# Last-layer MLP: a weight's high and low parts interleaved word by word, and the second up slab's product taken in another column order

## The chip, the cores and the metric

The kernel runs on one core of a Trainium2 chip. The metric is the device time of one execution in microseconds; lower is better.

## The reference

Two transformer layers run one after the other on 512 tokens of width 1024, in float32. The change touches only the end of the second layer, its squared-ReLU MLP with a hidden width of 4096:

```python
def squared_relu_mlp(xn, w_up, w_down):
    return jnp.square(jax.nn.relu(xn @ w_up)) @ w_down

x = x + squared_relu_mlp(rmsnorm_2(x, norm_mlp[l]), w_up[l], w_down[l])   # w_up 1024x4096, w_down 4096x1024
return rmsnorm_2(x, norm_final)
```

## The kernel before

Each operand of a product is split in a high part (`fp32r`, written by ScalarE as a Copy that rounds) and a low part (`fp32r`, VectorE: value minus high part). A product of a 128x128 weight block with a 128x512 activation block is then three matmuls into one PSUM bank (`mm3`, lines 902 to 904): high by high, high by low activation, low weight by high activation. Each matmul carries its own weight load.

Weights come in slabs of 1024x512 words (4096 words in each of the 128 partitions, 2 MB, two DMAs of 1 MB on SyncE's queue) into the two slots of `W` (`weight_slots`). A slab's slot is refilled when the slab two before it is used up. ScalarE then writes the high part in two halves of 2048 words into `W_hi` (`weights_hi`, arena tiles 0 to 15, two slots), and VectorE writes the low part in two halves into `W_lo` (`weight_slots_lo`, two slots). TensorE waits on the semaphore `w_lo` for both halves.

The last layer's MLP runs in MQ = 4 parts. `mlp_part` exists on TensorE, ScalarE and VectorE, and each part has four slabs, n = 0 to 3: two of `w_up` (8 blocks of 128 hidden features, MH = 8) and two of `w_down`. A slab is 4 output banks x KD = 8 blocks of the contraction x 3 matmuls = 96 matmuls, 1536 in all.

- n = 0 goes through `together` (lines 939, 940 and 944), which holds four banks open: first all products with the high activation, then those with the low one.
- n = 1 uses `mm3` with the activations `mlp_hi` and `xn_lo`. In the trace these are the rows of lines 902 to 904 with `mlp_hi` or `xn_lo`.
- n = 2 and 3 use `mm3` with `sq_hi` and `sq_lo`, the squares.

VectorE takes each up bank out of PSUM (line 3289: ReLU times `rstd`), ScalarE squares it into `sq_hi` (line 2399), VectorE squares it again and subtracts (`rsq`, `sq_lo`, lines 3291 and 3294), and adds each down bank to the residual (`part_out`, line 3302). The split of slab s+1 stands in the same program order on ScalarE (line 2394) and VectorE (line 3283): slab n+1 is split while TensorE works on slab n. The very first slab, `("mup", 0)`, is split earlier with `split_w` (lines 1664 and 2435), between the last residual additions of the attention. The DMA of the second slab waits for the job before `mup_0`, which is `norm_sum("norm_mlp")` (line 863), placed in the middle of the first slab's products.

Three lines elsewhere, which the change does not touch, use operands that are not contiguous or much narrower. `exponents` (lines 2925 to 2928, VectorE, levels `lev` = 2, 4, ... 128, twice each) works on views split into runs of `lev // 2` words:

```python
v = v.rearrange("p (n b t) -> p n b t", b=2, t=lev // 2)
return v[:, :, 0], v[:, :, 1]
...
V.tensor_tensor(Al, ref(Fc, 0, hp, lev), Fl, ALU.subtract)          # line 2925
```

so at `lev` = 2 both inputs and the output step by two words. Line 1027 (TensorE) reads its moving operand as `posT[0:33, :].rearrange("p (i e) -> p e i", e=2)[:, e, :]`, every second word; line 1034 reads a contiguous one. Line 1342 is a product with 128 contiguous moving columns and a contiguous 128x128 weight block in plain float32; the trace records two load and matmul pairs for each such product.

Of the kernel before, what the change touches and what calls it, by code (L numbers as in the profile page):

```python
# [13 lines left out]
F32 = mybir.dt.float32  # L14
# [335 lines left out]
def two_blocks(nc, io, out_dram):  # L350
# [10 lines left out]
    with ExitStack() as ctx:  # L361
# [192 lines left out]
        sq_lo, sq_hi = parts("sq_lo", 16, MH), parts("sq_hi", 32, MH)  # L554
# [278 lines left out]
        def _(pe):  # L833
# [776 lines left out]
            def mlp_part(first, q):  # L1610

                for n in range(4):
                    s = s0 + n
                    pe.wait_ge(w_lo, 2 * (w0 + n + 1) + 8 * first + 8 * q)
                    wh, wl = (w[:, s % 2, :].rearrange("p (k c) -> p k c", k=KD) for w in (W_hi, W_lo))
# [9 lines left out]
                    xh, xl = (mlp_hi, xn_lo) if n == 1 else (sq_hi, sq_lo)  # L1625
                    for m, j in enumerate(js):
                        c = slice(P * m, P * m + P)
                        pe.wait_ge(psum_free[j % 8], j // 8 + 2 * first + 2 * q)
                        for k in range(KD):
                            if n == 2 and m == 0:  # L1630

                                pe.wait_ge(sem("sq_lo"), k + 1 + MH * first + MH * q)
                            ins = mm3(PS[j % 8][:], wh[:, k, c], wl[:, k, c], xh[:, k, :], xl[:, k, :], k == 0, k == KD - 1)
                        ins.then_inc(psum_full, 1)
# [10 lines left out]
        def _(act):  # L1645
# [728 lines left out]
            def before_mlp(k):  # L2374
                if k:
                    high_mlp(k - 1)
                if k == KD - 2:
                    split_w("mup", 0)
                evicted(act, f"out3_{k}")
# [7 lines left out]
            def mlp_part(q, last):  # L2387

                for n in range(4):
                    if not (last and n == 3):  # L2390
                        s = s0 + n + 1
                        act.wait_ge(w_landed[s % 2], landings(s) + 64 * q)
                        for a, b in ((0, 2048), (2048, 4096)):
                            A(W_hi[:, s % 2, a:b], W[:, s % 2, a:b], ACT.Copy).then_inc(w_hi, 1)  # L2394
# [13 lines left out]
        def _(dve):  # L2408
# [854 lines left out]
            split_w("mup", 0)  # L3263
# [8 lines left out]
            def mlp_part(q, last):  # L3272


                for n in range(4):
# [3 lines left out]
                    if not (last and n == 3):  # L3279
                        s = s0 + n + 1  # L3280
                        for e, (a, b) in enumerate(((0, 2048), (2048, 4096))):
                            dve.wait_ge(w_hi, 2 * (w0 + n + 1) + e + 1 + 8 * q)
                            V.tensor_tensor(W_lo[:, s % 2, a:b], W[:, s % 2, a:b], W_hi[:, s % 2, a:b].bitcast(F32),  # L3283
                                            ALU.subtract).then_inc(w_lo, 1)
# [236 lines left out]
```

## Time and profile before

| | |
|---|---|
| median of 3 runs | 1660.04 us (1659.95 to 1660.29) |
| span of the profiled execution | 1660.1 us |
| TensorE matmuls busy | 1614.1 us (97%) |
| VectorE / ScalarE / GpSimd busy | 977.3 / 682.4 / 153.4 us |
| mean granted clock of TensorE | 0.993 |
| the four parts of the last MLP, first to last product | 1297.9 to about 1648 us |

The profiled execution has no other time than its span, and that is the median of the runs to 0.1 us. "PEld" rows are the weight loads, which overlap the matmuls. Matmul records overlap one another too: a record of 389 ns does not mean that one matmul starts every 389 ns. The distance from start to start is what counts.

### The profile page before, as it was taken

To read this page: it belongs to the slowest core of one execution; us is meant where nothing else is said; L and a number is where in the kernel's file an instruction comes from. 1 tells how busy PE (TensorE), PEld (TensorE's weight loads), DVE (VectorE), ACT (ScalarE), POOL (GpSimd) and SP (SyncE) were. 2 spreads that over 40 slices of the span, in tenths; PEclk is the share of its full clock that TensorE was granted. 3 is DMA by queue.
4 is the path that set the end of the run, shared out by engine and by line. 5 is a ranking of instruction groups with operands and counts; after the bars stand their busy time and mean duration, and the time that the engine had idled before them with its cause. 6 is when DMAs were issued, how large, how long until landed. Compare 5 with 4: busy or idle time off the path is not lost.

```text
span 1660.1 us, 18984 instructions
## 1 busy us (share of the span) xinstructions
PE 1614.1 (97%) x7258; PEld 1268.9 (76%) x7258; DVE 977.3 (59%) x1411; ACT 682.4 (41%) x1060; POOL 153.4 (9%) x155
## 2 busy tenths in 40 slices
PE   5999999999999999999999999999999999999997
PEld 1488765687788888888888787688877888888885
DVE  6986687784544424436789498675434554435262
ACT  4531465323533213325654667964433322222131
POOL 0221000252000000004000000342001000000001
PEclk9999999999999999999999999999999999999999
DMA  9543114422332232223141121444210322222231
GB/s 311 198 152 127 64 54 162 153 65 89 103 101 89 76 116 84 92 95 133 52 176 56 47 77 36 162 152 153 101 52 28 125 74 83 98 101 101 101 101 51
DMA packets 112600, 173.89 MB, mean 105 GB/s; under 512 B 3851, under 2 KB 56651, under 8 KB 112012
## 3 DMA queue, kind: packets, MB, share of 16 engines
q1 hardware_dynamic: 108220, 158.05, 28.2%
q0 software_dynamic: 4304, 14.81, 2.7%
q8 instruction: 49, 0.80, 0.2%
q14 instruction: 27, 0.22, 0.0%
HBM read 168.53 MB, written 4.33 MB: 104 GB/s over the span
## 4 chain that ended last, share of the span: by engine, by line
PE 84%; DVE 8%; DMA 3%; ACT 2%; issue 2%; SPq 1%; DVEq 0%; ACTq 0%
PE bank L902 17%; PE bank L904 17%; PE bank L903 17%; PE bank L939 6%; PE bank L940 6%; PE bank L944 5%; DMA weight_slots<-in_w_mod 2%; PE bank L1212 2%; PE bank L1132 1%; PE bank L1144 1%; PE bank L1342 1%; DVE weight_slots_lo L2435 1%; PE bank L1432 1%; PE bank L1407 1%; PE bank L1450 1%
## 5 line engine op out<-in xcount | busy, mean ns | idle before, releaser
L3328 POOL TENSOR_TENSOR arena<-arena 128x512 f32<-128x512 f32 (+1 forms) x56 | 76.3, 1371 | 960.3 <-ACT arena L1695 956.8
L904 PE MATMUL bank<-hx_hi,weight_slots_lo 128*128 128x512 f32 x320 | 124.8, 390 | 0.0
L3283 DVE TENSOR_TENSOR weight_slots_lo<-weight_slots,weights_hi 128x2048 fp32r<-128x2048 f32 x30 | 67.4, 2289 | 93.5 <-ACT weights_hi L2394 93.5
L2394 ACT ACTIVATE weights_hi<-weight_slots 128x2048 fp32r<-128x2048 f32 x30 | 55.8, 1908 | 160.6 <-DMA weight_slots<-in_w_up 115.9
L1664 ACT ACTIVATE weights_hi<-weight_slots 128x2048 fp32r<-128x2048 f32 (+2 forms) x46 | 77.3, 1724 | 91.7 <-DMA weight_slots<-in_ffn_w_down 57.9
L903 PE MATMUL bank<-xn_lo,weights_hi 128*128 128x512 f32 x288 | 112.0, 389 | 0.0
L902 PE MATMUL bank<-sq_hi,weights_hi 128*128 128x512 f32 x256 | 99.6, 389 | 0.0
L903 PE MATMUL bank<-sq_lo,weights_hi 128*128 128x512 f32 x256 | 99.6, 389 | 0.0
L904 PE MATMUL bank<-sq_hi,weight_slots_lo 128*128 128x512 f32 x256 | 99.6, 389 | 0.0
L1650 ACT ACTIVATE arena<-bank 128x512 f32<-128x512 f32 (+2 forms) x99 | 49.1, 532 | 96.1 <-PE bank L904 45.0
L2435 DVE TENSOR_TENSOR weight_slots_lo<-weight_slots,weights_hi 128x2048 fp32r<-128x2048 f32 (+2 forms) x34 | 65.8, 1973 | 28.1 <-ACT weights_hi L1664 28.1
L1695 ACT ACTIVATE arena<-arena 128x512 f32<-128x512 f32 (+1 forms) x68 | 38.9, 579 | 101.4 <-DVE arena L3302 28.3
L939 PE MATMUL bank<-xn_hi,weights_hi 128*128 128x512 f32 x192 | 76.3, 397 | 3.1 <-ACT xn_hi L1680 3.1
L2770 DVE TENSOR_TENSOR weight_slots_lo<-weight_slots,weights_hi 128x2048 fp32r<-128x2048 f32 x18 | 40.4, 2288 | 60.5 <-ACT weights_hi L1935 60.5
L940 PE MATMUL bank<-xn_hi,weight_slots_lo 128*128 128x512 f32 x192 | 75.9, 395 | 0.0
L944 PE MATMUL bank<-xn_lo,weights_hi 128*128 128x512 f32 x320 | 74.2, 389 | 0.0
L3302 DVE TENSOR_TENSOR arena<-bank,arena 128x512 f32<-128x512 f32 x32 | 22.1, 690 | 87.3 <-PE bank L904 87.3
L904 PEld LDWEIGHTS bank<-hx_hi,weight_slots_lo 128*128 128x128 f32 x320 | 60.1, 188 | 12.8
L944 PEld LDWEIGHTS bank<-xn_lo,weights_hi 128*128 128x128 f32 x320 | 60.1, 188 | 12.5
L902 PE MATMUL bank<-ff_hi,weights_hi 128*128 128x512 f32 x176 | 68.5, 389 | 0.0
L903 PE MATMUL bank<-ff_lo,weights_hi 128*128 128x512 f32 x176 | 68.5, 389 | 0.0
L904 PE MATMUL bank<-ff_hi,weight_slots_lo 128*128 128x512 f32 x176 | 68.5, 389 | 0.0
(473 smaller groups left out, 4069.6 us busy)
## 6 DMA issues: line engine op xcount, KB each, us to landing
weight_slots<-in_w_in SPq DMA_DIRECT2D x24, 1024.0 KB, 7.3
weight_slots<-in_ffn_w_up SPq DMA_DIRECT2D x22, 1024.0 KB, 6.8
weight_slots<-in_w_up SPq DMA_DIRECT2D x16, 1024.0 KB, 6.6
weight_slots<-in_w_down SPq DMA_DIRECT2D x16, 1024.0 KB, 6.4
weight_slots<-in_w_mod SPq DMA_DIRECT2D x14, 1024.0 KB, 10.2
arena<-in_w_mod POOLq DMA_DIRECT2D x32, 256.0 KB, 3.3
weight_slots<-in_w_out SPq DMA_DIRECT2D x8, 1024.0 KB, 7.8
weight_slots<-in_w_xkv SPq DMA_DIRECT2D x8, 1024.0 KB, 7.6
```

The costliest lines, as they stand in the source:

```text
L902: mm(ps, lh, rh, start=start, stop=False)
L903: mm(ps, lh, rl, start=False, stop=False)
L904: return mm(ps, ll, rh, start=False, stop=stop)
L939: mm(ps[:, 0:width], wh(k, m), x2[0][:, k, 0:width], start=k == 0, stop=False)
L940: mm(ps[:, 0:width], wl(k, m), x2[0][:, k, 0:width], start=False, stop=False)
L944: ins = mm(ps[:, 0:width], wh(k, m), x2[1][:, k, 0:width], start=False, stop=k == KD - 1)
L1650: free(A(out, src, ACT.Copy), name)
L1664: A(high_half(kind, n, i), W[:, s_, a:b], ACT.Copy).then_inc(w_hi, 1)
L2394: A(W_hi[:, s % 2, a:b], W[:, s % 2, a:b], ACT.Copy).then_inc(w_hi, 1)
L2435: V.tensor_tensor(low(kind, n)[:, a:b], W[:, s, a:b], high_half(kind, n, i).bitcast(F32), ALU.subtract).then_inc(w_lo, 1)
L3283: V.tensor_tensor(W_lo[:, s % 2, a:b], W[:, s % 2, a:b], W_hi[:, s % 2, a:b].bitcast(F32), ALU.subtract).then_inc(w_lo, 1)
L3328: G.tensor_tensor(acc, acc, sq[i % 2][:, 0:width], ALU.add).then_inc(sq_added, 1)
```

## The change

For the 16 slabs of this MLP, high and low part of a slab now lie in one tile `W_pair` of 4096 x 2 words: word 2i is the high part of weight i, word 2i + 1 its low part. There are two such tiles (for even and odd slots), in arena tiles 0 to 15 and 32 to 47. `sq_hi` moves from tiles 32 to 39 to tiles 24 to 31. ScalarE writes, and VectorE reads and writes, with a step of two words, and so does every weight load. `W_lo` is no longer used in this MLP. The order of instructions, the semaphores and their counts stay.

For the slabs n = 1, the moving operand and the PSUM output are both read in the order `p (a j b) -> p j a b` with a = 2, j = 64, b = 4: columns 0 to 3, 256 to 259, 4 to 7, 260 to 263 and so on. Each column still goes to its own place in the bank.

```diff
@@ -551,7 +551,10 @@
         pT = tiles(44, 2)
         pbuf = [tile(46), tile(47)]
         ao_lo, ao_hi = parts("ao_lo", 24, 8), parts("ao_hi", 16, 8)
-        sq_lo, sq_hi = parts("sq_lo", 16, MH), parts("sq_hi", 32, MH)
+        sq_lo, sq_hi = parts("sq_lo", 16, MH), parts("sq_hi", 24, MH)
+        first_pair = slabs["mup", 0][0] % 2
+        W_pair = [parts(f"weights_pair_{i}", 32 if i == first_pair else 0, 16).rearrange("p a c -> p (a c)").rearrange(
+            "p (w e) -> p w e", e=2) for i in range(2)]
         relu = [tile(a) for a in range(58, 62)]
         rsq = [tile(80), tile(81)]
 
@@ -1612,7 +1615,7 @@
                 for n in range(4):
                     s = s0 + n
                     pe.wait_ge(w_lo, 2 * (w0 + n + 1) + 8 * first + 8 * q)
-                    wh, wl = (w[:, s % 2, :].rearrange("p (k c) -> p k c", k=KD) for w in (W_hi, W_lo))
+                    wh, wl = (W_pair[s % 2][:, :, e].rearrange("p (k c) -> p k c", k=KD) for e in range(2))
                     js = [j0 + 4 * n + m for m in range(4)]
                     if n == 0:
                         for j in js:
@@ -1623,6 +1626,11 @@
                                  lambda: norm_sum("norm_mlp"), KD if first else 4)
                         continue
                     xh, xl = (mlp_hi, xn_lo) if n == 1 else (sq_hi, sq_lo)
+
+                    def turned(v, n_=n):
+
+                        return v.rearrange("p (a j b) -> p j a b", a=2, b=4) if n_ == 1 else v
+
                     for m, j in enumerate(js):
                         c = slice(P * m, P * m + P)
                         pe.wait_ge(psum_free[j % 8], j // 8 + 2 * first + 2 * q)
@@ -1630,7 +1638,7 @@
                             if n == 2 and m == 0:
 
                                 pe.wait_ge(sem("sq_lo"), k + 1 + MH * first + MH * q)
-                            ins = mm3(PS[j % 8][:], wh[:, k, c], wl[:, k, c], xh[:, k, :], xl[:, k, :], k == 0, k == KD - 1)
+                            ins = mm3(turned(PS[j % 8][:]), wh[:, k, c], wl[:, k, c], turned(xh[:, k, :]), turned(xl[:, k, :]), k == 0, k == KD - 1)
                         ins.then_inc(psum_full, 1)
 
             mlp_part(0, 0)
@@ -2375,7 +2383,10 @@
                 if k:
                     high_mlp(k - 1)
                 if k == KD - 2:
-                    split_w("mup", 0)
+                    s = slabs["mup", 0][0]
+                    act.wait_ge(w_landed[s % 2], landings(s))
+                    for a, b in ((0, 2048), (2048, 4096)):
+                        A(W_pair[s % 2][:, a:b, 0], W[:, s % 2, a:b], ACT.Copy).then_inc(w_hi, 1)
                 evicted(act, f"out3_{k}")
 
             norm_squares("norm_mlp", lambda k: xb[:, k, :], before=before_mlp)
@@ -2391,7 +2402,7 @@
                         s = s0 + n + 1
                         act.wait_ge(w_landed[s % 2], landings(s) + 64 * q)
                         for a, b in ((0, 2048), (2048, 4096)):
-                            A(W_hi[:, s % 2, a:b], W[:, s % 2, a:b], ACT.Copy).then_inc(w_hi, 1)
+                            A(W_pair[s % 2][:, a:b, 0], W[:, s % 2, a:b], ACT.Copy).then_inc(w_hi, 1)
                     for m in range(4 * n, 4 * n + 4) if n < 2 else ():
                         r = relu[m % 4]
                         j = j0 + m
@@ -3260,7 +3271,11 @@
             low_mlp([0, 1, 2, 3])
             residual("out3", [5])
             low_mlp([4])
-            split_w("mup", 0)
+            s = slabs["mup", 0][0]
+            for e, (a, b) in enumerate(((0, 2048), (2048, 4096))):
+                dve.wait_ge(w_hi, 2 * split_no["mup", 0] + e + 1)
+                pair = W_pair[s % 2][:, a:b, :]
+                V.tensor_tensor(pair[:, :, 1], W[:, s % 2, a:b], pair[:, :, 0].bitcast(F32), ALU.subtract).then_inc(w_lo, 1)
             residual("out3", [6])
             low_mlp([5])
             residual("out3", [7])
@@ -3280,8 +3295,8 @@
                         s = s0 + n + 1
                         for e, (a, b) in enumerate(((0, 2048), (2048, 4096))):
                             dve.wait_ge(w_hi, 2 * (w0 + n + 1) + e + 1 + 8 * q)
-                            V.tensor_tensor(W_lo[:, s % 2, a:b], W[:, s % 2, a:b], W_hi[:, s % 2, a:b].bitcast(F32),
-                                            ALU.subtract).then_inc(w_lo, 1)
+                            pair = W_pair[s % 2][:, a:b, :]
+                            V.tensor_tensor(pair[:, :, 1], W[:, s % 2, a:b], pair[:, :, 0].bitcast(F32), ALU.subtract).then_inc(w_lo, 1)
                     if n < 2:
                         for m in range(4 * n, 4 * n + 4):
                             j = j0 + m
```

## Rows read from the trace of the kernel before

**Rows 1.** The page, part 1: busy time, share and instructions of each engine.

```profile
span 1660.1 us, 18984 instructions
PE 1614.1 (97%) x7258; PEld 1268.9 (76%) x7258; DVE 977.3 (59%) x1411; ACT 682.4 (41%) x1060; POOL 153.4 (9%) x155
```

**Rows 2.** One MLP part in windows: length, busy of engines, clock, DMA share.

```profile
core 0: us, PE busy (x) PEld busy (x) DVE busy (x) ACT busy (x) POOL busy (x), PEclk, DMA share, GB/s
1387.00:1474.00 87.00, 87.00 (x386) 72.06 (x385) 39.36 (x41) 19.95 (x16) 0.00 (x0) 1.00 0.29 97
```

**Rows 3.** The chain that ended last, from 1270 us: start, duration, what.

```profile
1306.87 7.85 DMA weight_slots<-in_w_up
1314.75 1.93 ACT weights_hi L2394
1318.90 2.30 DVE weight_slots_lo L3283
...
1401.35 7.25 PE bank L944 x32
...
1575.43 7.25 PE bank L944 x32
```

**Rows 4.** Who waited for whom, TensorE from 1268 us: us, times, longest.

```profile
PE bank L902 <- DVE weight_slots_lo L3283: 0.6, 1, 0.6
```

**Rows 5.** Groups by line, form kept, in the window 1297 to 1650 us.

```profile
L902 PE MATMUL bank<-sq_hi,weights_hi 128*128 128x512 f32 x256 | 99.6, 389 | 0.0
L3283 DVE TENSOR_TENSOR weight_slots_lo<-weight_slots,weights_hi 128x2048 fp32r<-128x2048 f32 x30 | 67.4, 2289 | 93.5 <-ACT weights_hi L2394 93.5
L2394 ACT ACTIVATE weights_hi<-weight_slots 128x2048 fp32r<-128x2048 f32 x30 | 55.8, 1908 | 160.6 <-DMA weight_slots<-in_w_up 115.9 <-DMA weight_slots<-in_w_down 44.7
L902 PEld LDWEIGHTS bank<-sq_hi,weights_hi 128*128 128x128 f32 x256 | 48.1, 188 | 10.0
```

**Rows 6.** Timeline inside slab n = 1: start, duration, engine, line.

```profile
1324.12 0.39 PE L902 MATMUL bank<-mlp_hi,weights_hi 128*128 128x512 f32 x1
1324.12 0.19 PEld L903 LDWEIGHTS bank<-xn_lo,weights_hi 128*128 128x128 f32 x1
1324.35 0.39 PE L903 MATMUL bank<-xn_lo,weights_hi 128*128 128x512 f32 x1
```

**Rows 7.** Timeline of a run of 128-column matmuls, level products of the second layer.

```profile
930.54 1.95 PE L1342 MATMUL bank<-arena 128*128 128x128 f32 x16
930.54 1.75 PEld L1342 LDWEIGHTS bank<-arena 128*128 128x128 f32 x15
```

**Rows 8.** Timeline at the kernel's start: two runs of 256-column matmuls.

```profile
5.36 1.12 PE L1027 MATMUL bank<-arena 33*64 33x256 f32 x4 [5.36 <-DMA arena<-in_hy_w]
10.26 1.12 PE L1034 MATMUL bank<-arena 64*64 64x256 f32 x4 [3.78 <-ACT arena L1733]
```

**Rows 9.** Single lines of VectorE: duration min/median/max, first and last start.

```profile
L2925 DVE TENSOR_TENSOR arena<-arena x14: 676/685/696, 867.1 to 1010.1; 128x512 f32<-128x512 f32 x14
L3294 DVE TENSOR_TENSOR sq_lo<-arena,sq_hi x32: 691/693/696, 1322.6 to 1605.9; 128x512 fp32r<-128x512 f32 x32
```

**Rows 10.** Groups of shorter splits, whole kernel: 1024 words on each engine.

```profile
L2441 DVE TENSOR_TENSOR weight_slots_lo<-weight_slots,weight_slots_lo 128x1024 fp32r<-128x1024 f32 x12 | 14.7, 1222 | 7.3 <-ACT weight_slots_lo L1675 7.3
L1675 ACT ACTIVATE weight_slots_lo<-weight_slots 128x1024 fp32r<-128x1024 f32 x12 | 12.5, 1045 | 0.0
```

**Rows 11.** Timeline before the third up slab: its split, its first product.

```profile
1375.58 4.49 DVE L3283 TENSOR_TENSOR weight_slots_lo<-weight_slots,weights_hi 128x2048 fp32r<-128x2048 f32 x2 [4.33 <-ACT weights_hi L2394]
1386.68 0.39 PE L939 MATMUL bank<-mlp_hi,weights_hi 128*128 128x512 f32 x1
```

**Rows 12.** Timelines around the first slab: its split, and its first product.

```profile
1290.99 3.72 ACT L1664 ACTIVATE weights_hi<-weight_slots 128x2048 fp32r<-128x2048 f32 x2 [1.82 <-DMA weight_slots<-in_w_up]
1292.94 4.49 DVE L2435 TENSOR_TENSOR weight_slots_lo<-weight_slots,weights_hi 128x2048 fp32r<-128x2048 f32 x2 [4.39 <-ACT weights_hi L1664]
1297.87 0.39 PE L939 MATMUL bank<-mlp_hi,weights_hi 128*128 128x512 f32 x1
```


## The prediction, made before the changed kernel ran

> **What bounds the kernel now.** I read the page first: TensorE's matmuls are busy 97% of the span, no other engine above 59% [rows 1]. In the last layer TensorE is busy for the whole of an 87 us window, at a granted clock of 1.00, that is at 2.4 GHz; VectorE has 39 us of work there and ScalarE 20 [rows 2]. The chain that ended last says the same: the low products of slab n = 0 start at 1401.35 and 1575.43 us, two parts of 384 matmuls apart, so 174.08 / 768 = 226.7 ns from matmul to matmul [rows 3]. Nothing but TensorE's own pace is in those parts. Two places are otherwise: the start of the first slab, and the start of the second, where the chain leaves TensorE for the DMA of the slab (it lands at 1314.72), ScalarE's first half and VectorE's two halves [rows 3]. There TensorE waits 0.6 us, its only wait for a split in this layer [rows 4].
>
> So the change can cost time in two ways: by the pace of 1536 matmuls with their loads, or by the splits at those two places. It removes no instruction and no wait.
>
> **The groups and the pace.** One matmul record lasts 389 ns, one weight load 188 ns [rows 5]. The timeline shows how they lie: the load for the next matmul starts with the current matmul (1324.12), lasts 188 ns, and the next matmul starts at 1324.35 [rows 6]. The load is off the path by 226.7 - 188 = 38.7 ns, and the group's idle time agrees (10.0 us over 256 loads is 39 ns) [rows 5]. That is the cover of a slower load.
>
> **Weight loads with a step of two words (1536 of them).** No load in the trace has a step. From below: nothing to gain, since the load is hidden already. From above: a load that needs the time of every word it passes. Its streaming time comes from the 128-column products: 15 loads in 1.75 us from the first start to the last end, so (1.75 - 0.188) / 14 = 111.6 ns from load to load, with the 128-column matmuls between them, and a load streams in no more than that [rows 7]. The rest of its 188 ns is latency that does not repeat. Doubled, a load record would be 188 + 111.6 = 299.6 ns, past the matmul's 226.7 by 72.9 ns even if the next matmul starts the instant the load ends: 1536 x 72.9 = 112.0 us.
>
> Which end? A stepped load passes 2 x 128 words in 111.6 ns, 2.29 words per ns. The moving operand is read at 512 words in 226.7 ns, 2.26 words per ns [rows 3, 7]. Passing memory at that rate is what TensorE's other read does all the time. The nearest row with a step is a moving operand of every second word, line 1027: 4 records in 1.12 us, and the contiguous line 1034, of the same 256 columns, also 1.12 us [rows 8]. Other port, slow start of the kernel, but the step itself cost nothing. I take 0.
>
> **Turned order in the slabs n = 1 (4 slabs x 96 = 384 matmuls).** The moving operand is read, and the bank written, in 128 runs of four words that hop between the two halves of the 512. No row shows a matmul output that is not contiguous. From below 0: no row shows a 512-column product at a shorter pace than 226.7 ns, in whatever place its operands lie. From above: half pace, one more 226.7 ns for each matmul, 384 x 0.2267 = 87.1 us. In between: one lost column slot for each run, 128 x 226.7 / 512 = 56.7 ns a matmul, 21.8 us in all. The number of columns and of matmuls is the same, and the stepped read of line 1027 ran at the contiguous pace [rows 8]; a run of four is milder than a step of two. I take 0 and keep both prices for rivals.
>
> **ScalarE's and VectorE's splits (32 halves each).** VectorE: two inputs and an output with a step of two words occur at level 2 of line 2925; all its 14 executions, over seven levels, lie between 676 and 696 ns, the contiguous 512-word subtraction of line 3294 at 691 to 696 [rows 9]. So VectorE's step costs 0. ScalarE has no stepped write in the trace. From below 0; from above each word twice: 2048 words take 1.908 us and 1024 take 1.045, so 0.843 ns a word, and a half would take 1.73 us more [rows 5, 10]. I take 0, as on VectorE.
>
> What hides a slower split: at a later slab VectorE is done at 1375.58 + 4.49 = 1380.07 and TensorE starts the slab at 1386.68, 6.6 us of slack [rows 11]. At the first slab the split ends at 1292.94 + 4.49 = 1297.43 and the first product starts at 1297.87: 0.44 us of slack [rows 12]. At the second slab there is none, TensorE already waits [rows 4]. Of a split, ScalarE's first half and VectorE's two halves are in the chain. ScalarE doubled costs 1.73 - 0.44 = 1.3 us at the first slab and 1.7 us at the second, 3.0 us together: the DMA of the second slab waits for a job inside the first slab, so the shift carries on and the two add.
>
> **Edits at nothing.** The new homes of the pair tiles and of `sq_hi` only need dead memory; semaphores, their counts and the queues are the same, and no DMA moves. Two buffers alternate by slab parity as before, so no new wait arises.
>
> **Sum.** 0 + 0 + 0 against the profiled execution's own 1660.1 us, which is the runs' median: 1660.0 us. The changes that this kernel's measurement can tell from none are those over 0.2%, 3.3 us.
>
> **Rivals.**
>
> A. *The bank's write order sets the pace.* For: every PSUM write of the trace is contiguous, so nothing vouches for hops. Against: the same columns in the same number. At half pace 1660.0 + 87.1 = 1747.1 us; at one slot for each run 1681.8 us. It decides (over 0.2%) from 3.3 us / 384 = 8.6 ns a matmul on. Chance 0.11, of it 0.05 for the small price.
>
> The Trainium skill speaks against the change here (Advanced Engine Details and Errata, "PSUM Cachelines"): any non-contiguous pattern slows matmuls significantly. Its next line asks only that every two consecutive elements be contiguous, which runs of four fulfil. By the first line rival A holds and the sum goes by its price, up to 1747.1 us; by the second it stays at 1660.0. No row here shows which.
>
> B. *The stepped weight load outgrows its cover.* For: no stepped load in the trace. Against: the rates above. It decides beyond 38.7 + 3.3 / 1.536 = 40.8 ns more a load, a third of its streaming time. At twice the streaming time 1660.0 + 112.0 = 1772.0 us. Chance 0.06.
>
> C. *ScalarE's stepped write is slow.* 1663.0 us if doubled, just inside 0.2%. If VectorE doubled too (2.289 - 1.222 = 1.07 us for 1024 words, so 2.13 us a half), the chain would grow by 1.73 + 4.27 = 6.0 us, still under the 6.6 us of later slabs, and the end would come 5.6 + 6.0 = 11.6 us later, 1671.6 us; its own rows speak against that [rows 9, 10]. Chance 0.04, of it 0.03 within 0.2%.
>
> D. *Faster.* The only slack to win on the chain is the 0.6 us wait, 0.03%. A better placing of operands in memory could shorten the pace of 226.7 ns, but from 2.1 ns a matmul on it would show, and nothing in the window varies. Chance 0.02.
>
> **How the numbers follow.** Forecast, all costs hidden or nil: 0.77. With the small case of C, within 0.2%: 0.80. Slower: 0.11 + 0.06 + 0.01 = 0.18. Faster: 0.02. The range 1658.0 to 1665.0 holds the forecast and C's small case, 0.80; what it leaves out is A, B, C's large case and D. Reaching for A's small price at 1682 would add 0.05 for three times the width.
>
> **What the changed profile would show.** Right: the rows of lines 902 to 904 with `mlp_hi` at 389 ns, weight loads of the last layer at 188 ns with 39 ns of idle each, the low products of n = 0 again 87.04 us apart, the stepped ScalarE and VectorE halves at 1.91 and 2.29 us, 0.6 us of wait at the second slab. Wrong by A: longer matmul records in n = 1 alone, its parts 87 us plus a quarter of the excess. Wrong by B: load records above 227 ns and matmuls of all four slabs apart by as much, n = 2 and 3 too. Wrong by C: longer ScalarE halves and a longer wait at two places only.

## The result: slower by 1.1%

The changed kernel takes 1679.01 us (median; 1677.14 to 1679.21), the kernel before in the same comparison 1659.99 us (1658.47 to 1660.29). The ratio is 1.0111, with a 95% interval of 1.0099 to 1.0123: 19.0 us slower. The forecast was 1660.0 us, with 1665.0 as the upper end.

Part 1 of the page of the changed kernel, which answers to [rows 1]:

```profile
span 1677.2 us, 18984 instructions
PE 1632.6 (97%) x7258; PEld 1278.5 (76%) x7258; DVE 979.6 (58%) x1411; ACT 692.4 (41%) x1060; POOL 154.0 (9%) x155
```

The instructions are the same in number. In this pair of profiled executions TensorE is busy 18.5 us longer, ScalarE 10.0 and VectorE 2.3. The next question is whether the added TensorE time is waiting or pace. The chain that ended last, answering to [rows 3]:

```profile
1312.69 7.47 PE bank L947 x32
1404.56 7.47 PE bank L947 x32
1496.39 7.47 PE bank L947 x32
1588.21 7.47 PE bank L947 x32
```

(Lines 942, 943 and 947 here are lines 939, 940 and 944 of before; 905 to 907 are 902 to 904; ScalarE's split 2394 is 2405 and VectorE's 3283 is 3299.) The low products of n = 0 now stand 91.83 us apart instead of 87.04, 4.79 us more for a part, and a run of 32 takes 7.47 instead of 7.25 us. The first part loses 0.9 us less: from its first product to that of the second part it takes 92.71 us instead of 88.81. Its n = 0 is 0.6 us longer by the pace, and TensorE's wait for the split of the second slab, 0.6 us before [rows 4], is gone (only the load in front of it still waits, 0.2 us, last line of the groups below). From the first product of this MLP to the last it is 368.0 us instead of 349.7 in the two profiled executions, 18.3 us more. (Its first product comes at 1296.76 us against 1297.87; over the other runs that varies from 1295.1 to 1299.1 us.) The loss of 19.0 us, whose interval reaches from 16.4 to 20.4 us, thus lies in the last MLP. Between 1388 and 1476 us the window shows no idle time and the same clock as [rows 2], 1.00, which is 2.4 GHz:

```profile
core 0: us, PE busy (x) PEld busy (x) DVE busy (x) ACT busy (x) POOL busy (x), PEclk, DMA share, GB/s
1388.00:1476.00 88.00, 88.00 (x369) 71.27 (x369) 39.40 (x40) 22.47 (x16) 0.00 (x0) 1.00 0.27 96
```

The groups of the last layer (1297 to 1670 us), answering to [rows 5]:

```profile
L905 PE MATMUL bank<-sq_hi,weights_pair 128*128 128x512 f32 x256 | 100.9, 394 | 0.0
L3299 DVE TENSOR_TENSOR weights_pair<-weight_slots,weights_pair 128x2048 fp32r<-128x2048 f32 x30 | 69.9, 2374 | 97.6 <-ACT weights_pair L2405 97.6
L2405 ACT ACTIVATE weights_pair<-weight_slots 128x2048 fp32r<-128x2048 f32 x30 | 64.9, 2223 | 162.7 <-DMA weight_slots<-in_w_up 116.3 <-DMA weight_slots<-in_w_down 46.4
L905 PE MATMUL bank<-mlp_hi,weights_pair 128*128 128x512 f32 x128 | 53.7, 420 | 0.0
L905 PEld LDWEIGHTS bank<-sq_hi,weights_pair 128*128 128x128 f32 x256 | 49.4, 193 | 10.4
...
L905 PEld LDWEIGHTS bank<-mlp_hi,weights_pair 128*128 128x128 f32 x128 | 25.1, 196 | 7.8 <-DVE weights_pair L3299 0.2
```

The matmul records grow from 389 to 394 ns everywhere, and to 420 ns in n = 1. The weight load takes 193 instead of 188 ns and still has 41 ns of idle time behind it (10.4 us over 256). It is still shorter than its cover, and nevertheless the matmuls are further apart. The timeline at the border of n = 0 and n = 1, answering to [rows 6]:

```profile
1411.63 0.39 PE L947 MATMUL bank<-xn_lo,weights_pair 128*128 128x512 f32 x1
1411.87 0.42 PE L905 MATMUL bank<-mlp_hi,weights_pair 128*128 128x512 f32 x1
1412.12 0.42 PE L906 MATMUL bank<-xn_lo,weights_pair 128*128 128x512 f32 x1
1412.38 0.41 PE L907 MATMUL bank<-mlp_hi,weights_pair 128*128 128x512 f32 x1
1412.62 0.42 PE L905 MATMUL bank<-mlp_hi,weights_pair 128*128 128x512 f32 x1
```

The starts are 0.24 to 0.26 us apart. What I call the **pace** below is the distance of starts averaged over such rows: from the first to the 24th start of an output block of `mm3`, divided by 23, with the starts that the trace keeps to 1 ns (the views print them to 10). The first block of n = 1 in the first part, whose second start comes late, is left out here. Before, the pace is 226.7 ns in all four slabs (n = 0 is counted over its 32 low products). Now it is 233.3 ns in n = 0, 2 and 3 and 256.6 ns in n = 1. That is 4 x (3 x 96 x 6.6 + 96 x 29.9) ns = 19.1 us, and 18.2 us with the 0.9 us that the first part loses less.

ScalarE's and VectorE's halves are longer too. Two halves of each, first in the slab n = 1 and then in n = 2:

```profile
1419.91 5.00 ACT L2405 ACTIVATE weights_pair<-weight_slots 128x2048 fp32r<-128x2048 f32 x2 [5.87 <-DMA weight_slots<-in_w_down]
1446.08 4.07 ACT L2405 ACTIVATE weights_pair<-weight_slots 128x2048 fp32r<-128x2048 f32 x2 [8.03 <-DMA weight_slots<-in_w_down]
...
1422.46 5.12 DVE L3299 TENSOR_TENSOR weights_pair<-weight_slots,weights_pair 128x2048 fp32r<-128x2048 f32 x2 [7.63 <-ACT weights_pair L2405]
1448.18 4.49 DVE L3299 TENSOR_TENSOR weights_pair<-weight_slots,weights_pair 128x2048 fp32r<-128x2048 f32 x2 [5.19 <-ACT weights_pair L2405]
```

Before, a ScalarE pair took 3.72 us and a VectorE pair 4.49 us [rows 11, 12]. The step costs ScalarE 0.18 us a half and VectorE nothing. In the turned slab both are slower again, ScalarE by 0.9 and VectorE by 0.6 us a pair. All of this lies beside other work.

### The profile page after: what moved, and what is told of

It is laid out like the page before. It is cut to its first block, busy times and chain, and to the rows that moved or that the text cites. A ratio compares the mean times of both kernels' runs of the same rounds, so it can differ in the third digit from the quotient of the medians.

```text
span 1677.2 us, 18984 instructions
## 1 busy us (share of the span) xinstructions
PE 1632.6 (97%) x7258; PEld 1278.5 (76%) x7258; DVE 979.6 (58%) x1411; ACT 692.4 (41%) x1060; POOL 154.0 (9%) x155
## 4 chain that ended last, share of the span: by engine, by line
PE 87%; DVE 8%; DMA 2%; ACT 1%; issue 1%; SPq 1%; DVEq 0%; ACTq 0%
PE bank L905 17%; PE bank L907 17%; PE bank L906 17%; PE bank L942 6%; PE bank L943 6%; PE bank L947 5%; PE bank L1215 2%; PE bank L1135 1%; PE bank L1147 1%; PE bank L1065 1%; PE bank L1345 1%; PE bank L1435 1%; DMA weight_slots<-in_w_mod 1%; PE bank L1410 1%; DVE weight_slots_lo L2446 1%
## 5 line engine op out<-in xcount | busy, mean ns | idle before, releaser
L2405 ACT ACTIVATE weights_pair<-weight_slots 128x2048 fp32r<-128x2048 f32 x30 | 64.9, 2223 | 162.7 <-DMA weight_slots<-in_w_up 116.3
L3299 DVE TENSOR_TENSOR weights_pair<-weight_slots,weights_pair 128x2048 fp32r<-128x2048 f32 x30 | 69.9, 2374 | 97.6 <-ACT weights_pair L2405 97.6
L907 PE MATMUL bank<-hx_hi,weight_slots_lo 128*128 128x512 f32 x320 | 124.8, 390 | 0.0
L1672 ACT ACTIVATE weights_hi<-weight_slots 128x2048 fp32r<-128x2048 f32 (+2 forms) x44 | 73.6, 1715 | 88.9 <-DMA weight_slots<-in_ffn_w_down 57.2
L907 PE MATMUL bank<-sq_hi,weights_pair 128*128 128x512 f32 x256 | 100.9, 394 | 0.0
L905 PE MATMUL bank<-sq_hi,weights_pair 128*128 128x512 f32 x256 | 100.9, 394 | 0.0
L906 PE MATMUL bank<-sq_lo,weights_pair 128*128 128x512 f32 x256 | 100.9, 394 | 0.0
L942 PE MATMUL bank<-xn_hi,weights_hi 128*128 128x512 f32 x192 | 75.6, 394 | 3.1 <-ACT xn_hi L1688 3.1
L2781 DVE TENSOR_TENSOR weight_slots_lo<-weight_slots,weights_hi 128x2048 fp32r<-128x2048 f32 x18 | 40.4, 2288 | 59.7 <-ACT weights_hi L1943 59.7
L2446 DVE TENSOR_TENSOR weight_slots_lo<-weight_slots,weights_hi 128x2048 fp32r<-128x2048 f32 (+2 forms) x32 | 61.3, 1953 | 23.2 <-ACT weights_hi L1672 23.0
L905 PE MATMUL bank<-hx_hi,weight_slots_lo 128*128 128x512 f32 x160 | 64.7, 405 | 1.0 <-DVE weight_slots_lo L2452 1.0
L906 PE MATMUL bank<-hx_lo,weight_slots_lo 128*128 128x512 f32 x160 | 62.3, 389 | 0.0
L905 PE MATMUL bank<-xn_hi,weights_hi 128*128 128x512 f32 x160 | 62.2, 389 | 0.0
```

Source lines behind the costliest of these rows:

```text
L905: mm(ps, lh, rh, start=start, stop=False)
L906: mm(ps, lh, rl, start=False, stop=False)
L907: return mm(ps, ll, rh, start=False, stop=stop)
L942: mm(ps[:, 0:width], wh(k, m), x2[0][:, k, 0:width], start=k == 0, stop=False)
L1672: A(high_half(kind, n, i), W[:, s_, a:b], ACT.Copy).then_inc(w_hi, 1)
L2405: A(W_pair[s % 2][:, a:b, 0], W[:, s % 2, a:b], ACT.Copy).then_inc(w_hi, 1)
```

## The experiments

### One part at a time

**e1_pair_only**: the interleaved pair with everything that belongs to it, in plain column order.

```diff
-    ins = mm3(turned(PS[j % 8][:]), wh[:, k, c], wl[:, k, c], turned(xh[:, k, :]), turned(xl[:, k, :]), ...)
+    ins = mm3(PS[j % 8][:], wh[:, k, c], wl[:, k, c], xh[:, k, :], xl[:, k, :], ...)     # against the changed kernel
```

> The changed kernel with its second up slabs in the plain column order; only the word-by-word interleaving is left. In the changed kernel matmuls of slabs n = 0, 2, 3 follow one another every 233.3 ns, 6.6 ns more than before. Theory 'two separate costs, the stepped weight load in the path': all 1536 matmuls take 6.6 ns more, n = 1 too, so 1660.0 + 10.2 = 1670.2 us. Rival 'the interleaving only hurts through ScalarE and VectorE working on the same words': the pace is longer only where these two work. Rival 'the load is hidden as predicted, the turned slabs disturb the rest': 1660 us.

**e2_turned_only**: the turned order on the kernel before, with its separate high and low tiles.

```diff
-    ins = mm3(PS[j % 8][:], wh[:, k, c], wl[:, k, c], xh[:, k, :], xl[:, k, :], ...)
+    ins = mm3(turned(PS[j % 8][:]), wh[:, k, c], wl[:, k, c], turned(xh[:, k, :]), turned(xl[:, k, :]), ...)
```

> The kernel before with only the turned column order in the second up slabs; weights contiguous. In the changed kernel these 384 matmuls follow every 256.5 ns. Theory 'two separate costs that add': 256.5 - 6.6 = 249.9 ns each, 384 x 23.2 = 8.9 us more, 1668.9 us. Rival 'the slower of two sets the pace': 256.5 ns alone as well, 384 x 29.8 = 11.4 us more, 1671.4 us.

Measured: e1 1669.31 us, ratio 1.0051 (1.0037 to 1.0065); e2 1669.44 us, ratio 1.0056 (1.0043 to 1.0070). The kernel before on the same chip took 1660.76 us. The product of the two ratios is 1.0107; the whole change has 1.0111. The pace says where: in e1 it is 233.3 ns in every slab, in e2 250.1 ns in n = 1 and 226.7 ns elsewhere. So the two costs are 6.6 ns for each of 1536 matmuls (10.2 us) and 23.4 ns for each of 384 (9.0 us). They add up, also where they meet: 226.7 + 6.6 + 23.4 = 256.7, measured 256.6. Groups of e1:

```profile
L2405 ACT ACTIVATE weights_pair<-weight_slots 128x2048 fp32r<-128x2048 f32 x30 | 61.3, 2096 | 162.2 <-DMA weight_slots<-in_w_up 116.0 <-DMA weight_slots<-in_w_down 46.2
L905 PE MATMUL bank<-mlp_hi,weights_pair 128*128 128x512 f32 x128 | 50.5, 395 | 0.0
L905 PEld LDWEIGHTS bank<-mlp_hi,weights_pair 128*128 128x128 f32 x128 | 24.7, 193 | 5.5 <-DVE weights_pair L3299 0.3
```

and of e2:

```profile
L2398 ACT ACTIVATE weights_hi<-weight_slots 128x2048 fp32r<-128x2048 f32 x30 | 56.5, 1932 | 159.6 <-DMA weight_slots<-in_w_up 115.4 <-DMA weight_slots<-in_w_down 44.2
L902 PE MATMUL bank<-mlp_hi,weights_hi 128*128 128x512 f32 x128 | 53.3, 416 | 0.2 <-DVE weight_slots_lo L3287 0.2
L902 PEld LDWEIGHTS bank<-mlp_hi,weights_hi 128*128 128x128 f32 x128 | 24.2, 189 | 8.2 <-DVE weight_slots_lo L3287 0.6
```

In e2 the load record is as before (189 ns) while the matmul record has grown to 416: the turned order slows the matmul and not the load. ScalarE's split is slightly slower there too (1932 against 1908 ns) though its own operands are contiguous.

### Which side of the turned matmul: e3_turned_read, e4_turned_write

```diff
-    ins = mm3(PS[j % 8][:], wh[:, k, c], wl[:, k, c], xh[:, k, :], xl[:, k, :], ...)
+    ins = mm3(PS[j % 8][:], wh[:, k, c], wl[:, k, c], turned(xh[:, k, :]), turned(xl[:, k, :]), ...)   # e3
+    ins = mm3(turned(PS[j % 8][:]), wh[:, k, c], wl[:, k, c], xh[:, k, :], xl[:, k, :], ...)           # e4
```

> The kernel before, with only the moving operand of the second up slabs read in the turned order; the bank is written contiguously, so these slabs' columns land in other places. Theory 'the PSUM write of hopping runs costs' (rival A of the prediction): 226.7 ns as before, 1660.0 us. Rival 'the read of the moving operand costs': all of what the turned order costs, about 250 ns a matmul, 1669 us.

> The kernel before, with only the PSUM output of the second up slabs written in the turned order; the moving operand is read contiguously, so these slabs' columns land in other places. Theory 'the PSUM write costs': about 250 ns a matmul, 1669 us. Rival 'the read costs': 226.7 ns, 1660.0 us. If both sides cost a part, each of the two runs shows its part.

Measured: e3 1670.17 us, e4 1660.91 us, before 1660.76 us. The pace of n = 1 is 250.1 ns in e3, exactly e2's, and 226.7 ns in e4. The chain and the group of e4:

```profile
1400.37 7.25 PE bank L944 x32
1487.40 7.25 PE bank L944 x32
...
L902 PE MATMUL bank<-mlp_hi,weights_hi 128*128 128x512 f32 x128 | 49.9, 390 | 0.0
```

Its parts are 87.03 us apart, as in [rows 3]. Writing a bank in 128 hopping runs of four words is free; reading the moving operand so is the whole cost. Of the two lines of the Trainium skill that the prediction weighed (Advanced Engine Details and Errata, "PSUM Cachelines"), this measurement agrees with the second, on pairs of elements, and not with the first, on any non-contiguous pattern.

### What in the read costs: e7, e8, e11, e12

These change the order in which n = 1 reads its 512 moving words. They are e3 with other numbers in `p (a j b) -> p j a b`: runs of b words, taken in turn from a places.

```diff
+    v.rearrange("p (a j b) -> p j a b", a=64, b=4)            # e7: runs of 4, 32 bytes apart
+    v.rearrange("p (a j b) -> p j a b", a=2, b=8)             # e8: runs of 8, hop 1 KB
+    a, b = ((0, 0), (4, 4), (16, 4), (2, 0))[m]               # e11; m = 0: hop 1008 bytes, m = 3: every second word
+    a, b = ((2, 2), (2, 16), (2, 32), (2, 64))[m]             # e12: runs of 2, 16, 32, 64, hop 1 KB
```

> The kernel before, the moving operand of slabs n = 1 read in runs of four words at a distance of eight words, in two sweeps (the bank is written contiguously, columns land elsewhere). Again 128 runs, but no hop of 1 KB. Theory 'every break between runs costs': 250.1 ns a matmul, 1669 us. Rival 'the hop between the two halves, 1 KB apart, costs': 226.7 ns, 1660 us.

> The kernel before, the moving operand of slabs n = 1 read in runs of eight words that hop between the halves (64 runs; the bank is written contiguously). Theory 'every break between runs costs the same': half of 23.4 ns, 238.4 ns a matmul, 1664.5 us. Rival 'the three-dimensional pattern itself costs': 250.1 ns. Rival 'runs shorter than eight words are the trouble': 226.7 ns.

> The kernel before, moving operand of slabs n = 1 read in runs of four words in four ways, one for each output block (bank written contiguously, columns land elsewhere). m = 0: hops of 1008 bytes instead of 1024; m = 1: four places 512 bytes apart in turn; m = 2: sixteen places 128 bytes apart in turn; m = 3: no runs, every second word, in two sweeps. Theory 'two reads at a power-of-two distance meet in the same part of the memory': m = 0 near the 231.1 ns of the 32-byte distance, m = 1 and 2 at 250 ns or more. Rival 'any break costs by how far it jumps': m = 0 at 250.1, m = 1 below it, m = 2 near 231. m = 3: by the Trainium skill's rule of two accesses a line 226.7 ns; if every further line costs as in the weight load's case, 233 ns or more.

> The kernel before, moving operand of slabs n = 1 read in runs that hop between the halves, the run length by output block: 2, 16, 32 and 64 words for m = 0, 1, 2, 3 (256, 32, 16 and 8 runs; bank written contiguously, columns land elsewhere). Runs of four cost 23.4 ns a matmul (128 runs), runs of eight 16.6 (64 runs, 0.26 ns each). Theory 'a fixed cost for a hop that short runs partly hide': 16 words 32 x 0.26 = 8.3 ns, 235.0; 32 words 230.9; 64 words 228.8; 2 words above 250. Rival 'a three-dimensional pattern has a fixed cost beside it': the last three converge on a value above 226.7 ns.

Measured: e7 1662.25 us (before 1660.78), e8 1669.18 (1660.78), e11 1689.22 and e12 1671.88 (1659.99). The paces of n = 1, with what each is above 226.7 ns:

| run of words | distance of the runs | pace, ns | more |
|---|---|---|---|
| 4 | 32 bytes, ascending | 231.1 | 4.4 |
| 4 | 128 bytes, 16 places | 247.3 | 20.6 |
| 4 | 512 bytes, 4 places | 267.5 | 40.8 |
| 4 | 1008 bytes, 2 places | 243.2 | 16.5 |
| 4 | 1024 bytes, 2 places | 250.1 | 23.4 |
| 8 | 1024 bytes, 2 places | 243.3 | 16.6 |
| 16 / 32 / 64 | 1024 bytes, 2 places | 240.5 / 236.8 / 228.7 | 13.8 / 10.1 / 2.0 |
| 2 | 1024 bytes, 2 places | 339 | 112 |
| 1, every second word | 8 bytes | 450.7 | 224.0 |

(The 231.1 ns of e7 hold for parts 1 to 3; in its part 0 the pace is 233.3.) The last line of the table, seen in the timeline of e11 at the border of the blocks m = 2 and m = 3:

```profile
1431.62 0.42 PE L903 MATMUL bank<-xn_lo,weights_hi 128*128 128x512 f32 x1
1431.87 0.41 PE L904 MATMUL bank<-mlp_hi,weight_slots_lo 128*128 128x512 f32 x1
1432.12 0.62 PE L902 MATMUL bank<-mlp_hi,weights_hi 128*128 128x512 f32 x1
1432.56 0.63 PE L903 MATMUL bank<-xn_lo,weights_hi 128*128 128x512 f32 x1
```

A moving operand of every second word takes twice the time (450.7 / 226.7 = 1.99). This is the very pattern that the prediction took for free from line 1027. Runs of 4 words, which are 16 bytes, cost 2% at the shortest distance and 7 to 18% at the others; runs below 16 bytes cost half as much again or all of it again. Longer hopping runs cost less, but not in proportion to the number of hops: 128 runs cost 23.4 ns, 64 cost 16.6, 32 cost 13.8. No price per hop fits, and the sums written down before the runs missed: 238.4 ns for runs of 8 (243.3), 235.0 for 16 (240.5), 230.9 for 32 (236.8), while 228.8 for 64 came true (228.7); and at 1008 bytes either 231.1 or 250.1 (243.2). The Trainium skill (Advanced Engine Details and Errata, "SBUF Cachelines") wants at least two hits on a 16-byte line for full performance. For the moving operand this measurement differs: every second word has two hits on each line and takes twice the time.

### The stepped load: e5, e6, e10, e14

**e5_load_step4** leaves all writes of ScalarE and VectorE contiguous and lets TensorE alone read its weights with a step of four words. **e6_load_64** loads half as many weight columns. **e10_steps** reads with steps of 3, 4, 5 and 8 words in the four blocks of each slab.

```diff
+    def stepped(w, k, m):                                                   # e5, all four slabs
+        return w.rearrange("p (k c e) -> p k c e", k=KD, e=4)[:, k, :, m]
+    mm3(PS[j % 8][0:64, :], wh[:, k, P * m:P * m + 64], wl[:, k, P * m:P * m + 64], ...)     # e6, n = 1, 2, 3
+    def stepped(w, k, m, step):                                             # e10, e9, e13, e15
+        at = min(512 * k, 4096 - P * step)
+        return w[:, at:at + P * step].rearrange("p (c e) -> p c e", e=step)[:, :, 0]
+    sh, sl = (stepped(w, k, m, (3, 4, 5, 8)[m]) for w in wide)              # e10, n = 1, 2, 3
```

> The kernel before: ScalarE and VectorE write high and low parts contiguously as ever, but all 1536 weight loads of the MLP read their 128 words with a step of four (the hidden features come out in another order). Step two cost 6.6 ns a matmul. Theory 'the load pays by the distance it passes': three extra words for each where step two had one, 3 x 6.6 = 19.9 ns, 246.6 ns a matmul, 1690.6 us. Rival 'the loads only suffered from ScalarE and VectorE working word by word on the same tile': 226.7 ns, 1660 us. Rival 'what counts is how many words of a 16-byte line are used' (Trainium skill, SBUF): one of four is past its limit, a far larger cost than three times step two's.

> The kernel before, but the 1152 matmuls of slabs n = 1, 2, 3 load only 64 of their 128 weight columns (half of the output rows are left out). Theory 'the load is in the path, a matmul starts some 39 ns after its load has ended': the load is half its streaming time shorter, up to 55.8 ns, and the pace falls below 226.7 ns, until something else holds it; down to 213.3 ns (512 columns at 2.4 GHz) it would give 1152 x 13.4 = 15.4 us, 1644.6 us. Rival 'the matmul sets the pace and the load hides behind it, as predicted': 226.7 ns, 1660 us.

> The kernel before, loads in slabs n = 1, 2, 3 with a step of 3, 4, 5 and 8 words for output blocks m = 0, 1, 2, 3 (other weights than the reference's), tiles written contiguously. Theory 'from a step of four on every word is a line of its own and the load itself takes 235 ns': 235.0 ns for steps 4, 5 and 8, and between 233.3 and 235.0 for step 3. Rival 'the distance passed counts': more for 5 and more again for 8. Whole: about 1660.8 + 1152 x 0.0083 = 1670.4 us.

Measured: e5 1671.21 us and e6 1663.42 us against 1660.78; e10 1675.74 against 1659.99. Groups of e5:

```profile
L902 PE MATMUL bank<-mlp_hi,weights_hi 128*128 128x512 f32 x128 | 50.9, 398 | 0.0
L902 PEld LDWEIGHTS bank<-mlp_hi,weights_hi 128*128 128x128 f32 x128 | 39.6, 310 | 0.0
```

At a step of four words the load record is 310 ns with no idle time, and the pace is 234.9 ns, not the 246.6 that three times the price of step 2 would give. Here the load has outgrown its cover, as rival B had it, at a larger step: e15 below puts the load's own time at 233.3 ns. The steps 3, 4, 5 and 8 of e10 give 235.7, 235.2, 236.7 and 246.6 ns. Groups of e6:

```profile
L902 PE MATMUL bank<-mlp_hi,weights_hi 128*64 128x512 f32 x128 | 50.3, 393 | 0.2 <-DVE weight_slots_lo L3283 0.2
L902 PEld LDWEIGHTS bank<-mlp_hi,weights_hi 128*64 128x64 f32 x128 | 17.1, 134 | 12.8 <-DVE weight_slots_lo L3283 0.6
```

A load that is 54 ns shorter brings nothing: the pace is 230.0 ns, even 3.3 ns more, for which no run gives a reason. So the load of 188 ns is hidden, as [rows 5] had it.

**e14_blocks** keeps the shared tile and its two writers, but interleaves blocks of 128 words, so that every load is contiguous again; no turned order.

```diff
-            "p (w e) -> p w e", e=2) for i in range(2)]
+            "p (w e r) -> p w e r", e=2, r=P) for i in range(2)]
-    wh, wl = (W_pair[s % 2][:, :, e].rearrange("p (k c) -> p k c", k=KD) for e in range(2))
+    wh, wl = (W_pair[s % 2][:, :, e, :].rearrange("p (k m) r -> p k m r", k=KD) for e in range(2))
-    A(W_pair[s % 2][:, a:b, 0], W[:, s % 2, a:b], ACT.Copy).then_inc(w_hi, 1)
+    A(W_pair[s % 2][:, a // P:b // P, 0, :], W[:, s % 2, a:b].rearrange("p (w r) -> p w r", r=P), ACT.Copy).then_inc(w_hi, 1)
```

> High and low parts still interleaved in one tile, but in blocks of 128 words instead of word by word, and no turned order. If the word-by-word step is what costs, the second up slabs go back to 226.7 ns per matmul and the time to that of the kernel before (1660, ratio 1.000). If it is the sharing of one tile by both parts (both writers and both loads in the same rows), they stay at 233.3 ns and the time at 1669, as with the pair alone (ratio 1.005).

Measured: 1660.33 us against 1660.76, ratio 0.9999 (0.9990 to 1.0008). Its groups:

```profile
L2405 ACT ACTIVATE weights_pair<-weight_slots 128x2048 fp32r<-128x2048 f32 x30 | 55.8, 1909 | 159.4 <-DMA weight_slots<-in_w_up 113.3 <-DMA weight_slots<-in_w_down 46.1
L905 PE MATMUL bank<-mlp_hi,weights_pair 128*128 128x512 f32 x128 | 49.9, 390 | 0.0
L905 PEld LDWEIGHTS bank<-sq_hi,weights_pair 128*128 128x128 f32 x256 | 48.0, 188 | 9.9
```

All three are back at their old durations and the pace is 226.7 ns. The shared tile, its new place and the move of `sq_hi` cost nothing; the word step costs everything that e1 lost. e14 takes the step from the loads and from both writers at once. e9 below parts them: there the tiles are those of before, written contiguously, and in the slabs of 512 columns the blocks that load with a step of two run at 233.3 ns beside blocks at 226.7. So TensorE's own stepped load is enough. No version in the study that computes every column is faster than the kernel before.

### Why a hidden load costs: e9, e13, e15

The load keeps its 41 ns of idle time and the matmuls are 6.6 ns further apart. These three runs change the length of the matmul beside it.

```diff
+    N = 384 if n == 3 else 512                                 # e9: steps 1, 1, 2, 2 in the blocks m of n = 1, 2, 3
+    N = (256, 448, 480, 496)[m] if n == 3 else 512             # e13: step 1 in part 0, step 2 in parts 1 to 3
+    N = {1: (512,) * 4, 2: (256, 384, 448, 480), 3: (128, 256, 384, 448)}[n][m]     # e15
+    sh, sl = (stepped(w, k, m, {1: 1, 2: 4, 3: 8}[n] if first else 1) for w in wide)  # e15; parts 1 to 3 only
```

> The kernel before, loads changed in slabs n = 1, 2, 3 only, tiles written contiguously as before: output blocks m = 0, 1 load contiguously, m = 2, 3 with a step of two (other weights than the reference's). In slabs n = 3 only 384 of the 512 columns are computed. If the step alone explains the pair-only run, 512-column blocks run at 226.7 ns (m = 0, 1) and 233.3 ns (m = 2, 3); rival 'it was the place of the pair tile or the stepped writing': 226.7 ns for all four. With 384 columns the contiguous blocks should take 226.7 - 53.3 = 173.3 ns. Theory 'a stepped load adds a fixed time to each matmul': 180.0 ns for the stepped ones. Rival 'load and moving read get in each other's way all along': three quarters of 6.6 ns, 178.3 ns. Whole: 1660.8 + 3.8 - 20.5 = 1644 us.

> Layout of before. In parts 1 to 3 of the second up slabs the weight loads read every second word, in part 0 adjacent words; in the last of those slabs the four output blocks have 256, 448, 480 and 496 columns instead of 512 (other weight columns are used and columns are left out). If the stepped load costs because its own stream is too long for the matmul that covers it, the cost grows as the matmul gets shorter: more than 6.6 ns at 448, 480 and 496 columns, and largest at 256. If it costs through something that the 512-column read itself does (the two reads compete, or matmuls start only on a coarse grid), it is 6.6 ns at 512 columns, and anything between 0 and 6.6 at the shorter ones, 0 at 256 as it was at 384. Part 0 against parts 1 to 3 of the same block tells the two apart.

> Part 0 reads the weights contiguously; in parts 1 to 3 the loads of slab n = 2 read every fourth word and those of n = 3 every eighth. Columns of the four output blocks: 256, 384, 448, 480 in n = 2 and 128, 256, 384, 448 in n = 3, 512 in n = 1 (contiguous loads everywhere there; other weight columns are used and columns are left out). If a load at these steps needs 235 and 246 ns for itself, whatever the matmul does, every block of n = 2 stands at 235 ns and every block of n = 3 at 246 ns in parts 1 to 3, however few columns it has. If the loads are only delayed by the long matmul's own read, the short blocks are near their contiguous pace of part 0 (some 120 ns at 256 columns).

Measured: e9 1641.19 us, e13 1650.27, e15 1658.83, with fewer columns than before, so that only the paces count. In a block whose length differs from that of the block before it, the first starts still follow the old length (in e15 the first distance is 83 ns at 128 columns where the later ones are some 240). This table therefore counts from the third start of a block to the 24th, divided by 21 (ns; "1" is the contiguous load of the same run):

| columns | 1 | step 2 | step 4 | step 8 |
|---|---|---|---|---|
| 128 | 111.7 | | | 240.4 |
| 256 | 119.7 to 120.0 | 119.9 | 233.3 | 238 to 243 |
| 384 | 173.3 to 173.4 | 173.3 | 233.9 | 242 |
| 448 | 202.5 (e15: 206.7) | 203.6 | 237.4 | 245 |
| 480 | 216.7 (e15: 216.9) | 220.0 | 240.0 | |
| 496 | 223.4 | 225.1 | | |
| 512 | 226.7 | 233.3 | 235.2 (e10) | 246.7 (e10) |

(At 384 columns the first contiguous block of e9 stands at 174.6.) Two things are to be read off. At step 4 the pace is 233.3 ns and at step 8 it is 240 even beside matmuls that need 120 and 112 ns: that is the load's own time. The timeline of e15, two starts at 256 columns and step 4, then two at 128 columns and step 8 with their loads:

```profile
1420.25 0.39 PE L904 MATMUL bank<-sq_hi,weight_slots_lo 128*128 128x256 f32 x1
1420.48 0.39 PE L902 MATMUL bank<-sq_hi,weights_hi 128*128 128x256 f32 x1
...
1442.63 0.40 PE L903 MATMUL bank<-sq_lo,weights_hi 128*128 128x128 f32 x1
1442.87 0.40 PE L904 MATMUL bank<-sq_hi,weight_slots_lo 128*128 128x128 f32 x1
...
1442.56 0.34 PEld L903 LDWEIGHTS bank<-sq_lo,weights_hi 128*128 128x128 f32 x1
1442.80 0.34 PEld L904 LDWEIGHTS bank<-sq_hi,weight_slots_lo 128*128 128x128 f32 x1
```

At step 2 the load fits into 120 ns: at 256 columns stepped and contiguous loads keep the same pace. Stepped loads at 256 columns in e13:

```profile
1447.77 0.28 PE L903 MATMUL bank<-sq_lo,weights_hi 128*128 128x256 f32 x1
1447.89 0.28 PE L904 MATMUL bank<-sq_hi,weight_slots_lo 128*128 128x256 f32 x1
1448.01 0.28 PE L902 MATMUL bank<-sq_hi,weights_hi 128*128 128x256 f32 x1
```

So at 512 columns it has over 100 ns of room, and still costs 6.6 ns. Between the same blocks of one run the cost is 0 at 256 columns, 1.1 ns at 448, 3.3 at 480 and 1.7 at 496; at 384 columns, between neighbouring blocks of e9, it is 0, and at 512 it is 6.6. (Contiguous blocks of 448 columns differ by 4.2 ns between e13 and e15, where they are other blocks m of the slab, so the small values should not be taken as exact.) It does not grow as the cover shrinks, so "the load outgrows its cover" is refuted for step 2. It is no fixed addition to every matmul either (180.0 ns at 384 columns), nor a share of its length (178.3), the two sums written down before e9. The cost appears only beside a long read of the moving operand. That the two reads get in each other's way fits this, and it is argued, not shown.

## Why the prediction was wrong, step by step

- **What bounds the kernel**: right. TensorE's pace is all there is in the four parts, and the whole loss is 1536 matmuls at a slower pace (19.1 us by the paces, 19.0 by the medians; 18.3 from first to last product of the profiled executions).
- **"The load is off the path by 38.7 ns; that is the cover of a slower load"**: this is the first step that failed, by a wrong inference. The load did stay inside the cover (193 ns, 41 ns idle), the rates argued from [rows 7] held (a step-2 load fits in 120 ns), and rival B's mechanism did not occur. But idle time behind a load only proves that a longer load could fit, not that its reads leave the neighbour's reads alone. The term of 0 was 10.2 us. The mark that was set for rival B, 40.8 ns more a load, came from the same inference: 5 ns more on the load record went with 6.6 ns on every matmul, in all four slabs.
- **"A run of four is milder than a step of two", so the turned order costs 0**: the second step that failed. The comparison is even true (250.1 against 450.7 ns), but the row under it, line 1027, could not show the cost. Its float32 records run in two pairs, the second 0.46 us after the first, so each matmul reads its 256 words at 0.56 words per ns, and all four together at 0.91. Even in the middle of the kernel a contiguous float32 product of 256 columns starts only every 216 ns, 1.19 words per ns:

```profile
323.16 1.46 PE L1212 MATMUL bank<-arena 128*128 128x256 f32 x6
```

(One such record lasts 379 ns there, against 631 to 685 for line 1034 in [rows 8], and line 1144 (from 177 us), whose products also run in pairs, keeps 384 columns in 323 ns, again 1.19. TensorE was slower at the start of the kernel; the trace's clock record begins only at 18 us and does not say why.) The stepped read in e11 reaches 512 / 450.7 = 1.14 words per ns. Line 1027 stays below that rate, so a stepped read there has nothing to slow down, and even the float32 rows of the middle would lose only some 4% by it; the products of the last layer read 2.26 words per ns. That the rate is the reason is argued from these rows; no run changed it for line 1027 itself.

- **Rival A**: its mechanism, the bank's write order, is refuted by e4. Its place (n = 1 alone) and form (a longer matmul record) are what happened, on the read side, and its small price of 21.8 us is 2.4 times the 9.0 us measured. The rival named one of the two sides of the instruction that the edit turns; the other had been set to 0 by line 1027 and by the equal number of columns.
- **Rival C**: ScalarE's step costs 0.18 us a half, a tenth of the doubled price, and lies beside other work; VectorE's step costs nothing, as [rows 9] had it. Right as a cost held at nothing.
- **Placing of the tiles, and waits**: right. e14 measures both together at 0.9999, and TensorE's wait at the second slab is even gone.
- **Range**: rivals A and B were each given a price far above what happened, and the range stopped short of both. Costs between "nothing" and "one slot for each run" had no case of their own, and two of that size came together.

**Still open.** Why a step-2 load slows a 512-column matmul and not a 384-column one; why the hop cost is not monotonic in distance (4.4, 20.6, 40.8, 16.5, 23.4 ns); why contiguous blocks of 448 columns stand at 202.5 ns in one place and 206.7 in another. A rival to the clash of the two reads was written down before e13 and is not ruled out: that matmuls start only on a coarse raster of time, so that a small delay costs a whole step. Several steady paces are multiples of 6.67 ns (120.0, 173.3, 226.7 and 233.3 are 18, 26, 34 and 35 of them), and step 2 costs one such multiple at 512 columns; 216.7, 220.0 and 250.1 are none. One run that would bear on it, a stepped load beside a moving operand of narrower type, was not made.

## What to carry to other kernels

When TensorE's pace is the bound, a change of an access pattern on either of its reads is a cost until a row at the same pace, in the same type, shows otherwise; a row from a slow phase of the kernel shows nothing. Keep the moving operand in contiguous stretches, and interleave weights in blocks as long as a load (128 words, the only length tried) rather than word by word: e14 shares the tile for nothing. A gap behind a hidden instruction prices its length, not what it takes from its neighbours.

## What the runs showed of the hardware

- PSUM output in hopping runs of four words: no cost (226.7 ns).
- Moving operand in fp32r: every second word doubles the time (450.7 ns); runs of two words at a hop of 1 KB cost half as much again (339 ns); runs of four cost 4 to 41 ns, depending on the distance.
- Weight load of 128 columns: up to step 2 it fits in 120 ns, at step 4 it needs 233 ns, at step 8 240 ns.
- A hopping read by TensorE also slows the other engines: in the changed kernel's turned slab ScalarE's two halves take 5.00 instead of 4.07 us and VectorE's 5.12 instead of 4.49 us. With contiguous splits ScalarE's halves in that slab take some 2.0 us instead of 1.91 (e2, and e3 with the hopping read alone; in e4, with the hopping write alone, they stay at 1.91), VectorE's stay at 2.29.
- A load of 64 columns instead of 128 makes the pace slightly worse (230.0 ns).
